# Wider staging buffers for the weight load, casts divided over ScalarE and VectorE, and own slots for the two halves of a sample column

## The reference

```python
h = rmsnorm(x, g_norm)
z = h @ w_in                                  # w_in: 1024 x 5888
u_f, gate_f, qkv_na, gate_na, q_ca, gate_ca, g_merge = split(z)
y_f  = (fourier_mix(u_f) * silu(gate_f)) @ w_f_out      # Re(FFT2 over positions, group channels)
y_na = (neighborhood_attention(qkv_na) * silu(gate_na)) @ w_na_out
y_ca = (memory_attention(q_ca, rmsnorm(mem) @ w_mem_kv) * silu(gate_ca)) @ w_ca_out
merged = sum_b sigmoid(g_b) * y_b
y = rmsnorm(x + merged @ w_out, g_final)
```

## Time and profile before

| what | us |
|---|---|
| median of the 2 runs shown | 5479.87 (5420.02 and 5539.72) |
| the profiled execution, device time | 5421.13 |
| its span, from the first to the last instruction of the slowest core (core 3) | 5419.6 |
| the other cores' spans | 5407.2 to 5414.5 |

### The profile page before, as it was taken

The page is one execution under the profiler, slowest core; times in us unless marked ns, Lnnn a source line. Parts: engine busy times, 40 slices in busy tenths (PEclk is TensorE's granted clock), DMA queues, the critical chain, the costliest instruction groups (busy, mean ns, idle before and its releaser), DMA issues.

```text
span 5419.6 us, 117229 instructions; the slowest of 8 cores (5407.2 to 5419.6 us)
## 1 busy us (share of the span) xinstructions
PE 4650.1 (86%) x40768; PEld 2770.2 (51%) x40768; DVE 2930.3 (54%) x5765; ACT 2444.9 (45%) x5022; POOL 214.3 (4%) x403
## 2 busy tenths in 40 slices
PE   5967763149999999999999998999999899999998
PEld 3644442025555555555555555555555455555554
DVE  4785564225555555555555554555555545555554
ACT  4613422224544444454444444444444444445443
POOL 1100100000000000000000000000000000000000
PEclk9999997579999999999999998999999999999999
DMA  4504404721111111111111111111111111111111
GB/s 134 158 21 122 114 26 123 230 72 51 55 55 51 51 51 55 51 55 55 51 51 52 54 47 50 51 51 52 53 52 56 42 54 51 52 57 52 51 43 38
DMA packets 126183, 350.72 MB, mean 65 GB/s; under 512 B 13648, under 2 KB 48432, under 8 KB 125616
## 3 DMA queue, kind: packets, MB, share of 16 engines
q1 hardware_dynamic: 125616, 343.22, 19.6%
HBM read 263.47 MB, written 79.69 MB: 63 GB/s over the span
## 4 chain that ended last, share of the span: by engine, by line
PE 67%; DVE 6%; issue 3%; ACT 3%; DVEq 0%; DMA 0%; ACTq 0%; POOL 0%; POOLq 0%
PE pB L705 25%; PE pS L830 7%; PE pA L705 7%; PE pA L711 6%; PE pB L849 4%; PE pS L849 4%; PE pT L711 3%; PE pS L762 3%; DVE th L836 3%; PE pT L705 3%; ACT mT L844 2%; PE pT L843 2%; PE pT L459 1%; DVE mrg L840 1%; PE pT L720 1%
## 5 line engine op out<-in xcount | busy, mean ns | idle before, releaser
L705 PE MATMUL pB<-Win,hT 128*128 128x512 bf16 x6144 | 1452.6, 379 | 8.5 <-ACT th L828 6.8
L705 PEld LDWEIGHTS pB<-Win,hT 128*128 128x128 bf16 x6144 | 569.7, 98 | 602.5 <-issue 14.3
L828 ACT ACTIVATE th<-pB 128x512 f32<-128x512 f32 x768 | 458.5, 597 | 774.2 <-PE pB L705 464.9
L705 PE MATMUL pA<-Win,hT 128*128 128x384 bf16 (+1 forms) x3072 | 520.3, 313 | 2.2 <-ACT NT L721 2.0
L768 DVE TENSOR_TENSOR Pn<-Pn,Tint 128x768 bf16<-128x768 bf16 x580 | 315.1, 556 | 248.7 <-ACT Pn L767 246.0
L836 DVE SCALAR_TENSOR_TENSOR th<-th,pS 128x512 f32<-128x512 f32 x512 | 350.7, 685 | 160.2 <-PE pS L830 154.8
L459 PE MATMUL pT<-ident,xn 128*128 128x128 bf16 x1584 | 123.5, 222 | 307.4 <-DVE xn L457 150.0
L454 ACT ACTIVATE xn<-xe 128x1024 bf16<-128x1024 f32 x262 | 276.8, 1057 | 243.4 <-PE pT L459 119.8
L705 PEld LDWEIGHTS pA<-Win,hT 128*128 128x128 bf16 x3072 | 282.0, 99 | 159.0 <-issue 11.6
L766 ACT ACTIVATE Pn<-pS 128x384 bf16<-128x384 f32 x628 | 294.7, 490 | 121.7 <-PE pS L762 121.7
L767 ACT ACTIVATE Pn<-pS 128x384 bf16<-128x384 f32 x628 | 308.2, 491 | 65.8 <-PE pS L762 45.3
(11 more groups left out here) (150 smaller groups left out, 7174.8 us busy)
## 6 DMA issues: line engine op xcount, KB each, us to landing
xe<-xp SPq DMA_DIRECT2D x128, 512.0 KB, 3.5
xe<-xs SPq DMA_DIRECT2D x128, 256.0 KB, 3.7
xl<-xp SPq DMA_DIRECT2D x64, 512.0 KB, 3.3
yp<-xl SPq DMA_DIRECT2D x64, 512.0 KB, 2.7
xe<-xs SPq DMA_DIRECT2D x64, 512.0 KB, 3.4
xl<-xs SPq DMA_DIRECT2D x64, 512.0 KB, 3.3
ys<-xl SPq DMA_DIRECT2D x64, 512.0 KB, 2.7
ybuf<-yscr SPq DMA_DIRECT2D x128, 96.0 KB, 1.9
```

Of the source, the lines that this page charges most:

```text
L705: T.op('pe', lambda e, k=k: e.matmul(dstbank[:, 0:n], lhsT=hTt[:, k, :], rhs=Win[:, k, col:col + n], start=(k == 0), stop=(k == 7)), reads ...
L828: T.op('act', lambda e, th2=th2: e.activation(out=th2[:, :], in_=pB[:, :], func=AF.Tanh, scale=0.5), reads=['pB'], writes=[thn])
```

## The change

Three things are changed together.

- **Weight staging.** In the block of `es2a` three staging buffers of 2752 float32 columns take the place of four of 1536, and the chunk width follows (`stg_w`). So w_in goes in 16 transfers of 128 x 2752 instead of 32, all others (1024 and 512 columns wide) keep their size. A landed chunk is cast in pieces of at most 1408 columns that alternate between ScalarE and VectorE, so a chunk of 2752 is cast by both (1408 and 1344 columns); a chunk of 1024 or 512 is one piece, on ScalarE from buffers 0 and 2 and on VectorE from buffer 1.
- **Slots of the weights.** A weight's casts write `name + '_a'` on ScalarE and `name + '_d'` on VectorE, so that casts of different engines no longer wait for each other. Readers in the same `emit()` name both.
- **Sample columns.** The two half loads of a column write slots `xeNa` and `xeNb`, each with a semaphore of its own, so the second no longer waits for the first. Square and scaling read both. For the prompt one load writes both slots.

```diff
+        stg_w = [1536]
...
-            T.op('act', lambda e: e.activation(out=xn[:], in_=xt[:], func=AF.Square, scale=1.0 / 32, accum_out=ss[:]), reads=[xslot], writes=[xnn, ssn])
+            T.op('act', lambda e: e.activation(out=xn[:], in_=xt[:], func=AF.Square, scale=1.0 / 32, accum_out=ss[:]), reads=xs_, writes=[xnn, ssn])
...
         def load_weight(dst, src, nk, ncols, name, scale_t=None, scale_c=None, col0=0):
+            cw = stg_w[0]
             for k in range(nk):
                 o = 0
                 while o < ncols:
-                    w = min(1536, ncols - o)
+                    w = min(cw, ncols - o)
                     bi = lw_ctr[0] % n_stg[0]
                     lw_ctr[0] += 1
                     stg = stg_h[bi]
                     sn = 'stg%d' % bi
                     T.dma('sp', stg[:, 0:w], src[k * 128:(k + 1) * 128, col0 + o:col0 + o + w], sn, writes=[sn])
-                    if bi % 2 == 0:
-                        if scale_t is not None:
-                            T.op('act', lambda e, k=k, o=o, w=w, stg=stg: e.activation(out=dst[:, k, o:o + w], in_=stg[:, 0:w], func=AF.Copy, scale=scale_t[:, k:k + 1]), reads=[sn, 'gn', 'gmm'], writes=[name])
...
+                    po = 0
+                    pi = 0
+                    while po < w:
+                        pw = min(1408, w - po)
+                        eng = 'act' if (pi + bi) % 2 == 0 else 'dve'
+                        pi += 1
+                        oo = o + po
+                        if eng == 'act':
+                            if scale_t is not None:
+                                T.op('act', lambda e, k=k, oo=oo, po=po, pw=pw, stg=stg: e.activation(out=dst[:, k, oo:oo + pw], in_=stg[:, po:po + pw], func=AF.Copy, scale=scale_t[:, k:k + 1]), reads=[sn, 'gn', 'gmm'], writes=[name + '_a'])
...
+                                T.op('dve', lambda e, k=k, oo=oo, po=po, pw=pw, stg=stg: e.tensor_scalar(out=dst[:, k, oo:oo + pw], in0=stg[:, po:po + pw], scalar1=scale_t[:, k:k + 1], scalar2=None, op0=ALU.mult), reads=[sn, 'gn', 'gmm'], writes=[name + '_d'])
...
-                        T.dma('sp', xt[:], xp_c[c], xslot, writes=[xslot])
+                        T.dma('sp', xt[:], xp_c[c], xslot + 'a', writes=[xslot + 'a', xslot + 'b'])
...
-                        T.dma('sp', xt[0:64, :], xs_c[0, c], xslot, writes=[xslot])
-                        T.dma('sp', xt[64:128, :], xs_c[1, c], xslot, writes=[xslot])
+                        T.dma('sp', xt[0:64, :], xs_c[0, c], xslot + 'a', writes=[xslot + 'a'])
+                        T.dma('sp', xt[64:128, :], xs_c[1, c], xslot + 'b', writes=[xslot + 'b'])
...
-                stg = sb2a("stg2", [128, 1536], F32)
+                stg = sb2a("stg2", [128, 2752], F32)
                 stg_h[0] = stg
-                stg_h[1] = sb2a("stg2b", [128, 1536], F32)
-                stg_h[2] = sb2a("stg2c", [128, 1536], F32)
-                stg_h[3] = sb2a("stg2d", [128, 1536], F32)
-                n_stg[0] = 4
+                stg_h[1] = sb2a("stg2b", [128, 2752], F32)
+                stg_h[2] = sb2a("stg2c", [128, 2752], F32)
+                n_stg[0] = 3
+                stg_w[0] = 2752
```

More of the change, by code:

```diff
@@ L451, in rms_to_hT @@
                 ptv = pT
+            xs_ = xslot if isinstance(xslot, list) else [xslot]
             xn, ss, ssp, rstd = xn_l[par], ss_l[par], ssp_l[par], rstd_l[par]
             xnn, ssn, sspn, rsn = xn_names[par], 'ss%d' % par, 'ssp%d' % par, 'rstd%d' % par
-            T.op('act', lambda e: e.activation(out=xn[:], in_=xt[:], func=AF.Square, scale=1.0 / 32, accum_out=ss[:]), reads=[xslot], writes=[xnn, ssn])
+            T.op('act', lambda e: e.activation(out=xn[:], in_=xt[:], func=AF.Square, scale=1.0 / 32, accum_out=ss[:]), reads=xs_, writes=[xnn, ssn])
             T.op('dve', lambda e: e.tensor_scalar(out=ssp[:], in0=ss[:], scalar1=EPS, scalar2=None, op0=ALU.add), reads=[ssn], writes=[sspn])
             T.op('pool', lambda e: e.tensor_tensor(out=rstd[:], in0=ssp[:], in1=mh[:], op=ALU.pow), reads=[sspn, 'mh'], writes=[rsn])
-            T.op('dve', lambda e: e.tensor_scalar(out=xn[:], in0=xt[:], scalar1=rstd[:, 0:1], scalar2=None, op0=ALU.mult), reads=[xslot, rsn], writes=[xnn])
+            T.op('dve', lambda e: e.tensor_scalar(out=xn[:], in0=xt[:], scalar1=rstd[:, 0:1], scalar2=None, op0=ALU.mult), reads=xs_ + [rsn], writes=[xnn])
             for k in range(8):
@@ L476, in load_weight @@
                     T.dma('sp', stg[:, 0:w], src[k * 128:(k + 1) * 128, col0 + o:col0 + o + w], sn, writes=[sn])
-                    if bi % 2 == 0:
-                        if scale_t is not None:
-                            T.op('act', lambda e, k=k, o=o, w=w, stg=stg: e.activation(out=dst[:, k, o:o + w], in_=stg[:, 0:w], func=AF.Copy, scale=scale_t[:, k:k + 1]), reads=[sn, 'gn', 'gmm'], writes=[name])
-                        else:
[L481 to L488, removed]
@@ new lines, in load_weight @@
+                    po = 0
[8 more added lines that the diff above has]
+                                T.op('act', lambda e, k=k, oo=oo, po=po, pw=pw, stg=stg: e.activation(out=dst[:, k, oo:oo + pw], in_=stg[:, po:po + pw], func=AF.Copy, scale=scale_t[:, k:k + 1]), reads=[sn, 'gn', 'gmm'], writes=[name + '_a'])
+                            else:
+                                sc = 1.0 if scale_c is None else float(scale_c)
+                                T.op('act', lambda e, k=k, oo=oo, po=po, pw=pw, stg=stg, sc=sc: e.activation(out=dst[:, k, oo:oo + pw], in_=stg[:, po:po + pw], func=AF.Copy, scale=sc), reads=[sn], writes=[name + '_a'])
+                        else:
+                            if scale_t is not None:
+                                T.op('dve', lambda e, k=k, oo=oo, po=po, pw=pw, stg=stg: e.tensor_scalar(out=dst[:, k, oo:oo + pw], in0=stg[:, po:po + pw], scalar1=scale_t[:, k:k + 1], scalar2=None, op0=ALU.mult), reads=[sn, 'gn', 'gmm'], writes=[name + '_d'])
+                            else:
+                                sc = 1.0 if scale_c is None else float(scale_c)
+                                T.op('dve', lambda e, k=k, oo=oo, po=po, pw=pw, stg=stg, sc=sc: e.tensor_scalar(out=dst[:, k, oo:oo + pw], in0=stg[:, po:po + pw], scalar1=sc, scalar2=None, op0=ALU.mult), reads=[sn], writes=[name + '_d'])
+                        po += pw
@@ L519, in build_nc @@
                     for g in range(4):
-                        T.op('pe', lambda e, k=k, g=g: e.transpose(out=pT[0:96, g, :], in_=Wf1[:, k, g * 96:(g + 1) * 96], identity=ident[:]), reads=['Wf1', 'ident'], writes=['pT'], signal=(g == 3))
+                        T.op('pe', lambda e, k=k, g=g: e.transpose(out=pT[0:96, g, :], in_=Wf1[:, k, g * 96:(g + 1) * 96], identity=ident[:]), reads=['Wf1_a', 'Wf1_d', 'ident'], writes=['pT'], signal=(g == 3))
                     T.op('act', lambda e: e.activation(out=WfT[:], in_=pT[0:96, 0:4, :], func=AF.Copy), reads=['pT'], writes=['WfT'])
@@ L666, in build_nc @@
                             T.op('pe', lambda e, hp=hp, k=k: e.matmul(pA[:, 0:256], lhsT=Wkv_t[:, k, hp * 128:(hp + 1) * 128], rhs=memT[:, k, :], start=(k == 0), stop=(k == 7)),
-                                 reads=['memT', 'Wkv'], writes=['pA'], signal=(k == 7))
+                                 reads=['memT', 'Wkv_a', 'Wkv_d'], writes=['pA'], signal=(k == 7))
                         T.op('act', lambda e, hp=hp, KmT=KmT: e.activation(out=KmT[:, hp, :], in_=pA[:, 0:256], func=AF.Copy), reads=['pA'], writes=['KmT%d' % mi])
```

4 lines of the change are left out of this document (2 added, 2 removed).

## The result

The change makes the kernel a little faster, by much more than the measurement is uncertain and by less than I forecast. The median of its 11 runs is 5386.84 us against 5628.75 us of 10 runs of the kernel before. Both medians hold executions in which a die was slowed by up to hundreds of us whatever the kernel; the comparisons leave those out: ratio 0.9887, 95% interval 0.9854 to 0.992. The lowest executions are 5348.35 and 5419.06 us, 71 us apart, and the profiled one is 5349.12 us (span 5347.6) against 5421.13. In a second timing the ratio was 0.9875 (0.9858 to 0.9893).

The account below looks back on a forecast made before the run. The main loop was taken as largest but unchanged; sample columns were bound by one load landing per column, staging by transfer. Columns -84 and staging -3 + 3 = 0 took 5421.1 to 5337 us, range 5305 to 5405 (8 in 10).

Parts of the forecast that it names:

- the yardstick: Whole kernel: about 2% (108 us) is what a measurement can tell from no change; 84 us is 1.6%.
- the buffers: Weight staging, 24 small chunks: three buffers instead of four cost +3 us, from 0 to +15.
- the columns: Sample columns: own slots for the half loads take 84 us off, range 74 to 94.
- what binds the sample columns: Sample columns: one landing per column on SyncE's queue, 4.8 us worked out against 4.66 measured.
- The fit of the Trainium skill: Sample columns: transfer takes 2.0 us plus bytes over 436 KB per us; own slots would bring some 40 us.
- The halves do not collide: Rival denied here, sample columns: half loads together land later, losing 27 of the 84 us: 5364; 7 in 100.
- the stop: Early sample columns: 13 us without a store while eight `yscr` writes fill the DMA engines; forecast to stay.
- the other way round: Sample columns, second estimate: prompt stage's 196 + 13 + 2.5 = 211.5 us against 293 gives 81 off.
- the chosen way: Sample columns: 58.8 columns at 3.03 us take 178 us, 86 less; minus 2.5 gives 84 off.
- the width and the casts: Weight staging: wider w_in loads gain 3 us (0 to 7); casts on both engines, slots apart, gain nothing.
- the rival built on the fixed part: Weight staging: unhidden fixed 2.0 us a load; 16 loads fewer save 32 us: 5305; 12 in 100 with milder form.
- The rival in single file: Weight staging: refills waiting for casts hold later refills on SyncE's queue, +116 us, 5453 in all; 4 in 100.

## Why the prediction was wrong, and where it was right

**Failed: the yardstick.** "About 2% (108 us) is what a measurement of this kernel can tell from no change." It isn't: the interval of the ratio is 0.3% to either side, and the four lowest executions of the kernel before lie between 5419.06 and 5425.25 us. I took the 120 us between the two runs shown for the noise of the measurement, when the profiled execution at 5421.13, within 1.2 us of the lower one, already said how well a time repeats. The median shown was no base either: against it my 5337 read as 2.6% less, and the comparison gives 1.1%. A change forecast at 1.6% was a clear gain, and I should have called it one. In the sum two terms failed, the buffers and the columns, both below.

**Right: what binds the sample columns.** One landing per column on a queue that holds everything behind it. With the wait gone the period fell from 4.66 to 3.16 us, TensorE became the bound, SyncE waits for a free buffer, and the DMA share is 0.67 for the 0.68 worked out. The stage was to end at 648 us, and the last stores start at 648.1; that it agrees so closely is luck, as on this core the stage began 3 us sooner than forecast and took 3 us longer. The fit of the Trainium skill (DMA: Bandwidth & Descriptors, the anatomy of one DMA) was rightly set aside: with its 2.6 us to land, own slots would have brought 40 us, and they brought 74 to 78. The page gives it for transfers issued from GpSimd, and these are SyncE's. The halves do not collide (landings 4.0 us in the median, 3.7 before), and one load instead of two saves only 1 us.

**Mis-sized: the columns, by the period and by the stop.** I had the other way round, prompt stage plus stop plus slow clock, at 211.5 us, and it came to 217.2; the burst costs 19 to 20 us where I counted 13 + 2.5. By the chosen way, 58.8 columns at 3.03 us, they ran at 3.16 us in the middle of the stage, which is 7.6 us. The 3.03 was too low from the start: it came from one window of 100 us, while the prompt stage takes 3.11 us a column from its first store to its last (196.1 us for 63 steps), and that alone is 5 us. Against that stands an earlier start of the stage, 434.5 to 430.5 us, which I hadn't priced; every kernel with separate or single loads has it, so it comes from the loads too. Together 78 us at the end of the stage, for 84.

**Mis-sized: three buffers instead of four.** This is the step that failed by most: +3 us taken, +12.6 measured (8.5 for the 16 chunks, 4.1 for w_kv), inside my range of 0 to +15. The step was "Most of the 5.7 is queueing behind the other three, so the lower end is nearer". I took the landing of a load alone, 3.5 us, for a ring of three, and so a turn of 4.9. With three buffers the landing fell from 5.7 to 4.8 us in the median, not to 3.5, and even with two it is 4.3. Between landing and cast and between cast and next issue a chunk then waits 0.3 us each, 0.7 together, where I had 0.35 for the hops, which no row showed (0.3 with the four buffers of before). The turn is 6.6 to 6.8 us, near my upper bound of 7.1. Why a landing among two others takes 4.8 us when one alone takes 3.5 stays open.

**Right: the width and the casts.** w_in took 81 us for 83, but kernels with the old width took 80.7 to 83.0, and the share was at 1.0 in its middle already. The waits between casts (21 us) lay under the transfer and brought nothing that shows: with one slot a weight again, the staging is the same within 1.4 us. The rule of the Trainium skill to batch transfers to 1 MiB (DMA: Bandwidth & Descriptors, on bandwidth) and the rival built on the fixed part are both answered by this: with three or more of w_in's transfers in flight, of 0.46 to 1.41 MB, the fixed part is hidden. For chunks of 0.52 MB three in flight don't hide it. The rival in single file didn't come, the share in the whole staging was 0.83.

**The sum.** Forecast 84 us, measured 67 by the medians over the cores (72 by the profiled executions, 5421 to 5349). Of the 17 that are missing, 10 are the buffers and 6 the columns; the small rests go both ways.

## What to carry to other kernels

Where a tracker knows only names, two transfers into halves of one tile are a hidden chain: each costs a full landing (3.0 to 3.7 us here) times the loop count, and giving the halves names and semaphores of their own was worth 78 us in one place and 36 in another. Price a ring of buffers by the measured turn over their number, with the landing as it is with its neighbours in flight. Widening a chunk is no substitute for a buffer once every other load keeps its size. A burst of writes ahead of the loads on one queue stopped the engines for 15 us here; spread over the loop, the same writes cost nothing that shows.

## What the runs showed of the hardware

- Chunks of 512 KB with a cast behind each landed in 4.3, 4.8, 5.6 and 8.1 us (medians) from rings of two, three, four and six buffers, at a DMA share of 0.62, 0.70, 0.85 and 1.00.
- A load of 256 KB landed no sooner than one of 512 KB outside the staging (3.7 and 3.5 us).
- Two loads into 64 partitions each, in flight together, were within 1 us as fast as one into 128: 217.1 and 216.1 us for the stage.
- Eight writes of 768 KB in a row kept SyncE issuing for 15.9 us (up to 3.9 us a write, 0.38 when spread) and held the loads behind them. The engines stopped for 15 us at a DMA share of 0.95, and TensorE's granted clock fell to 0.59 of full speed in the mean of these 15 us, between its two levels of 1.2 and 2.4 GHz, after TensorE had run out of work. Spread over the columns they cost TensorE nothing (99.5 of 100 us busy, clock 1.00, DMA share 0.67).
